# First layer of a two-layer decoder trunk: load order, x in half slices, Q/K order of two heads, and the head output on another engine

## The reference

```python
# layer 1, mLSTM: 8 heads, DK 128, DV 256, SEQ 2048, D_MODEL 2048
u = x @ w_in                                   # q,k | v | o | z | i,f gates
qk = silu(causal_depthwise_conv(qk, conv_w, conv_b))
ig, fg = split(gates + gate_b);  lf = log_sigmoid(fg)
h = mlstm_chunkwise(q, k * DK**-0.5, v, ig, lf)     # C_t = f_t C_{t-1} + i_t k_t v_t^T, running-max stabiliser
h = (h - mean(h)) * rsqrt(var(h) + eps)             # per head
h = sigmoid(o) * (h * head_g) * silu(z)
x = layernorm(ALPHA * x + h @ w_out)
# layer 2, stick-breaking attention, 16 heads of 128, K/V and Q/gate projected from x
A[t,s] = sigmoid(z_ts) * prod_{s<j<t} (1 - sigmoid(z_tj)),  s < t
x = layernorm(ALPHA * x + (A @ v * silu(z)) @ w_out)
```

## Time and profile before

| what | value |
|---|---|
| times of three runs | 2713.29, 2716.52, 2899.35 us (median 2716.52) |
| profiled execution | 2710.15 us; its slowest core's span 2708.5 us |
| PE busy | 2554.2 us (94%), 13315 matmuls |
| DVE, ACT, POOL busy | 1602.8, 970.2, 1144.7 us |
| first matmul | 25.4 us |
| last V/o/z matmuls of layer 1 start | 1055.1 us |
| out-projection of layer 1 until about | 1283 us |
| a head of layer 2 | about 72.4 us |

### The profile page before, as it was taken

How to read it: one execution, slowest core, us unless ns; L and a number is a source line. 1 busy time by engine, 2 the same in 40 slices (tenths; PEclk the granted TensorE clock), 3 DMA queues, 4 the chain that set the end, 5 groups by cost and what they waited for, 6 DMA issues and landing times.

```text
span 2708.5 us, 38664 instructions; the slowest of 8 cores (2682.8 to 2708.5 us)
## 1 busy us (share of the span) xinstructions
PE 2554.2 (94%) x13315; PEld 1279.5 (47%) x13315; DVE 1602.8 (59%) x2676; ACT 970.2 (36%) x1829; POOL 1144.7 (42%) x1127
## 2 busy tenths in 40 slices
PE   4998989998999999999889999999999999999997
PEld 2564545554555565444334444444444444444443
DVE  2654545554555554665556666666666666666665
ACT  1533434343434442322333333444444343331111
POOL 2343434343434432433444444455544544443433
PEclk9998989999999999999999999999999999999999
DMA  9847576856657357796454555455454445566851
GB/s 166 135 75 112 81 107 90 113 86 96 105 91 115 62 135 154 194 239 186 92 114 99 106 107 109 105 113 103 101 111 107 101 107 112 131 164 177 260 208 78
DMA packets 472878, 335.06 MB, mean 124 GB/s; under 512 B 413424, under 2 KB 446320, under 8 KB 461168
## 3 DMA queue, kind: packets, MB, share of 16 engines
q1 hardware_dynamic: 452128, 198.30, 31.6%
q0 software_dynamic: 20560, 134.30, 28.2%
HBM read 273.86 MB, written 92.27 MB: 135 GB/s over the span
## 4 chain that ended last, share of the span: by engine, by line
PE 73%; DVE 9%; DMA 8%; issue 4%; POOL 3%; ACT 2%; SPq 1%; another core or an unknown queue 0%; DVEq 0%; ACTq 0%; POOLq 0%
PE PSA L860 26%; PE PSA L531 19%; PE PSA L699 12%; PE PSA L482 7%; DMA mida<-REGW 6%; DVE REGW L968 6%; PE PSA L1026 4%; PE PSA L941 3%; DMA REGX<-REGW 1%; POOL REGW L724 1%; DMA REGX<-x_t 1%; DVE REGW L867 1%; SPq L161 1%; DVE REGW L509 1%; PE PSA L586 0%
## 5 line engine op out<-in xcount | busy, mean ns | idle before, releaser
L860 PE MATMUL PSA<-REGH,REGX 128*128 128x512 bf16 x4096 | 976.1, 380 | 5.7 <-DVE REGW L867 5.7
L968 DVE TENSOR_TENSOR_SCAN REGW<-PSA,REGW 128x512 f32<-128x512 f32 (+3 forms) x640 | 684.3, 1091 | 286.2 <-ACT PSA L946 236.6
L531 PE MATMUL PSA<-REGH,REGX 128*128 128x256 bf16 (+1 forms) x4096 | 718.0, 331 | 2.9 <-DMA REGH<-a_wv 2.9
L994 POOL TENSOR_TENSOR REGW<-REGW 128x1024 bf16<-128x1024 f32 (+7 forms) x384 | 527.3, 1388 | 397.6 <-DMA REGX<-REGW 197.2
L860 PEld LDWEIGHTS PSA<-REGH,REGX 128*128 128x128 bf16 x4096 | 397.3, 98 | 460.3 <-issue 10.6
L531 PEld LDWEIGHTS PSA<-REGH,REGX 128*128 128x128 bf16 x4096 | 401.2, 99 | 243.9 <-issue 24.5
L946 ACT ACTIVATE PSA<-PSA 128x512 f32<-128x512 f32 (+3 forms) x640 | 326.7, 520 | 312.2 <-PE PSA L941 307.3
L482 PE MATMUL PSA<-REGX,REGH 128*128 128x512 bf16 x1024 | 242.4, 391 | 36.9 <-DMA REGX<-x_t 29.0
L941 PE MATMUL PSA<-REGW 128*128 128x512 bf16 (+3 forms) x640 | 222.0, 349 | 27.6 <-DVE REGW L968 27.4
L509 DVE SCALAR_TENSOR_TENSOR REGW<-REGW,PRT 128x512 f32<-128x512 f32 x192 | 151.4, 791 | 157.3 <-ACT REGW L504 153.2
L872 ACT CAST REGW<-PSA 128x512 bf16<-128x512 f32 x192 | 112.7, 587 | 346.7 <-PE PSA L860 344.8
(11 more groups left out here) (115 smaller groups left out, 1990.4 us busy)
## 6 DMA issues: line engine op xcount, KB each, us to landing
REGX<-wb POOLq DMA_DIRECT2D x64, 512.0 KB, 4.9
y<-REGW SPq DMA_DIRECT2D x26, 1024.0 KB, 4.4
REGH<-a_wv POOLq DMA_DIRECT2D x32, 768.0 KB, 19.4
wb<-kv_w POOLq DMA_DIRECT2D x32, 512.0 KB, 8.7
wb<-b_w_in POOLq DMA_DIRECT2D x32, 512.0 KB, 7.3
REGW<-y SPq DMA_DIRECT2D x14, 1024.0 KB, 7.5
REGW<-x SPq DMA_DIRECT2D x13, 1024.0 KB, 5.9
REGH<-a_wqk POOLq DMA_DIRECT2D x16, 512.0 KB, 27.5
```

The costliest lines, as they stand in the source:

```text
L531: yield Op("pe", lambda: P_.matmul(PS[bank][:, 0:n1 - n0], lhsT=XT[tb][:, c, t0:t0 + 128], rhs=WV[par][:, c, n0:n1], start=(c == 0), stop= ...
L860: yield Op("pe", lambda c=c: P_.matmul(PS[bank], lhsT=WS[i % 4][:, c, :], rhs=X1[tb][:, c, :], start=(c == 0), stop=(c == KC - 1)), R=[f"W ...
L968: yield Op("dve", lambda: V.tensor_tensor_scan(out=RR[slot][:, lo:hi][:, ::-1], data0=PS[bank][:, 0:w][:, ::-1], data1=mk[:, ::-1], initia ...
L994: yield Op("pool", lambda: G.tensor_tensor(out=AA[:, (pos + b0) * 128:(pos + b1) * 128], in0=RR[slot][:, lo + 1:hi + 1], in1=RR[slot][:, l ...
```

## The change

It touches the first layer's streams and, through planner costs, the order in both layers.

- **Load order.** POOL issues the first Q weights, x slice 0 and three more Q/K weights first, and only then its constants, which become a stream `consts`. Both heads' Q/K weights precede x slices 1 to 3. The `WV` block of head 1 is loaded only after the 16 Q/K blocks of heads 0 and 1 have been through the convolution, because four more convolution buffers `U` now lie in its place.
- **x in half slices.** Each x slice is two DMAs of 1 MB with a key each.
- **Q/K order.** For heads 0 and 1 the order is x slice by x slice: q and k of head 0, then of head 1 (`border`). The gate matmuls of slice 1, 2 and 3 stand ahead of that slice's blocks.
- **Gate weight column.** Column 256 of PSUM bank 0 is set to 1.0 once; the scaling of v then covers 257 columns, and the one-column copy goes.
- **Norm weight folded.** POOL's second multiplication goes. `HB` is made by DVE, as `HN * s * HG` in one operation, instead of by ACT; there are eight `HB` buffers instead of three.
- **Planner costs** of some twenty operations change by small amounts, those of the scan and of the subtraction of layer 2 among them.

```diff
-        kb.op("pool", lambda: G.memset(ONE32[:], 1.0), W=["ONE32"])
...
-        xtk = [[("XT", i)] for i in range(4)]
+        xtk = [[("XT", i, j) for j in range(2)] for i in range(4)]
...
-        HB = [wt(0.5, [256], BF16, [("HB", i)]) for i in range(3)]
+        HB = [wt(0.5, [256], BF16, [("HB", i)]) for i in range(8)]
...
+        U += [tile("H", 40 + 2.0625 * i, [528], F32, [("U", 4 + i)]) for i in range(4)]
+
+        def consts():
+            yield lambda: at("first") >= 0
+            yield Op("pool", lambda: G.memset(ONE32[:], 1.0), W=["ONE32"], cost=0.2)
...
+            yield Op("dve", lambda: V.memset(PS[0][:, 256:257], 1.0), W=[("ps", 0)], cost=0.1)
...
+            yield lambda: at("xt") >= 3
+            yield Op("sp", None, W=["HG"], cost=2.5, dma=dict(slot="hg", out=HG, in_=a_head_g.partition_broadcast(128)))
...
             def xt(tb):
-                yield Op("pool", None, W=xtk[tb], cost=10.5, dma=dict(slot=f"xt{tb}", out=XT[tb], in_=x_t[tb]))
+                for j in range(2):
+                    yield Op("pool", None, W=[xtk[tb][j]], cost=6.2,
+                             dma=dict(slot=f"xt{tb}{j}", out=XT[tb][:, 8 * j:8 * j + 8, :], in_=x_t[tb, :, 8 * j:8 * j + 8, :]))
                 st["xt"] = tb
+            yield from wq(0, 0)
+            yield from xt(0)
             yield Op("pool", None, W=["WG"], cost=0.4,
                      dma=dict(slot="wg", out=WG.rearrange("p a b -> p (a b)"), in_=a_wg))
-            yield from wq(0, 0)
-            yield from xt(0)
-            yield from wq(0, 1)
+            for i in range(1, 4):
+                yield from wq(i // 2, i % 2)
+            st["first"] = 0
             for tb in range(1, 4):
                 yield from xt(tb)
-            yield from wq(1, 0)
-            yield from wq(1, 1)
             yield from wv(0)
+            yield lambda: len(cvd) >= 16
             yield from wv(1)
...
+        border = [(h, tb, k) for tb in range(4) for h in range(2) for k in range(2)]
+        border += [(h, tb, k) for h in range(2, NH_A) for tb in range(4) for k in range(2)]
...
-                yield Op("act", lambda: A_.activation(out=v[:, 0:256], in_=PS[0][:, 0:256], func=AF.Copy, scale=w),
-                         R=[("ps", 0), "WW"], W=[("VX", i % 4)], cost=0.42, first=True)
-                st["vev"] = i
-                yield Op("act", lambda: A_.copy(out=v[:, 256:257], in_=w), R=["WW"], W=[("VX", i % 4)], cost=0.2, first=True)
+                yield Op("act", lambda: A_.activation(out=v[:, 0:257], in_=PS[0][:, 0:257], func=AF.Copy, scale=w),
+                         R=[("ps", 0), "WW"], W=[("VX", i % 4)], cost=0.48, first=True)
...
-                yield Op("pool", lambda: G.tensor_tensor(out=gg, in0=gg, in1=HG[:, 256 * h:256 * h + 256], op=ALU.mult),
-                         R=["HG"], W=[("GG", i % 3)], cost=0.6)
...
-                yield Op("act", lambda: A_.activation(out=HB[i % 3], in_=HN[q], func=AF.Copy, scale=s(3)),
-                         R=[("HN", q), sk(3)], W=[("HB", i % 3)], cost=0.36)
-                yield Op("sp", None, R=[("HB", i % 3)], W=[("MIDA", t, h)], cost=0.5,
...
+                yield Op("dve", lambda: V.scalar_tensor_tensor(out=HB[i % 8], in0=HN[q], scalar=s(3),
+                                                               in1=HG[:, 256 * h:256 * h + 256], op0=ALU.mult, op1=ALU.mult),
+                         R=[("HN", q), sk(3), "HG"], W=[("HB", i % 8)], cost=0.5, slack=0.4)
+                yield Op("sp", None, R=[("HB", i % 8)], W=[("MIDA", t, h)], cost=0.5,
...
-                        cost=0.12 + w * 0.0022)
+                        cost=0.22 + w * 0.00209)
```

More of the change, by code:

```diff
@@ L417, in prologue @@
             for tb in range(4):
-                yield lambda: at("xt") >= tb
+                yield lambda: at("xt") >= tb and at("const") >= 0 and at("qkp") >= 4 * tb - 1
+                if tb == 0:
+                    yield lambda: at("qkp") >= 3
                 for t in range(4 * tb, 4 * tb + 4):
@@ L423, in prologue @@
                                                          start=(c == 0), stop=(c == KC - 1)),
-                                 R=xtk[tb] + ["WG"], W=[("ps", 5)], inc=(c == KC - 1 and t % 4 == 3), cost=0.05, slack=0.5)
+                                 R=[xtk[tb][c // 8], "WG"], W=[("ps", 5)], inc=(c == KC - 1 and t % 4 == 3), cost=0.05, slack=0.3)
+                st["gates"] = tb
             g3 = PS[5][:, 0:256].rearrange("p (t g) -> p t g", g=16)
@@ L472, in prologue @@
             st["pro"] = 0
+        border = [(h, tb, k) for tb in range(4) for h in range(2) for k in range(2)]
+        border += [(h, tb, k) for h in range(2, NH_A) for tb in range(4) for k in range(2)]
+        cvd = set()
         def qkp():
-            for b in range(8 * NH_A):
-                h, tb, kind = b // 8, (b % 8) // 2, b % 2
+            for b, (h, tb, kind) in enumerate(border):
                 yield lambda: (at("xt") >= tb and at("wq") >= 2 * h + kind and at("ev") >= b - 2
-                               and (h < 2 or (at("recm") >= 16 * (h - 1) - 1 and at("vz") >= 16 * (h - 1) + 2 * (b % 8) - 2)))
+                               and (h < 2 or (at("recm") >= 16 * (h - 1) - 1 and at("vz") >= b - 2 + 16 * (h - 1) - 8 * h + b - 8 * h)))
+                if b % 4 == 0 and h < 2:
+                    yield lambda: at("gates") >= tb or tb == 0
                 i = 2 * (h % 2) + kind
@@ L489, in conv @@
         def conv(kind):
-            for b in range(kind, 8 * NH_A, 2):
-                h, tb = b // 8, (b % 8) // 2
-                yield lambda: at("qkp") >= b
+            for b, (h, tb, k_) in enumerate(border):
+                if k_ != kind:
+                    continue
+                yield lambda: at("qkp") >= b and at("prt") >= 0
                 par, bank, ch = h % 2, 3 + b % 2, 8 * kind + h
-                u, p = kind + 2 * (tb % 2), kind + 2 * ((tb + 1) % 2)
+                base = 4 if h == 1 else 0
+                u, p = base + kind + 2 * (tb % 2), base + kind + 2 * ((tb + 1) % 2)
                 acc, sig, ak, gk = ACC[kind], SIG[kind], [("ACC", kind)], [("SIG", kind)]
                 wk = lambda k: PRT[:, k * 16 + ch:k * 16 + ch + 1]
-                if tb == 0 and h > 0:
+                if tb == 0 and h > 1:
                     yield Op("pool", lambda: G.memset(U[u][:, 0:3], 0.0), W=[("U", u)], cost=0.1)
@@ L519, in conv @@
                                       in_=KTa[par][:, tb * 512:(tb + 1) * 512], transpose=True))
-                st["qk" if not kind else "kk"] = 4 * h + tb
+                cvd.add((h, kind, tb))
         def vzp():
@@ L606, in recm @@
                                                           scale=DB[:, col + 8:col + 9]), R=["C32", "DB"], W=[("CB", (i + 1) % 2)],
-                             cost=0.42, first=True)
+                             cost=0.52, first=True)
                 st["recm"] = i
@@ L613, in reco @@
                 b, q, col = 5 + i % 2, i % 2, 8 * t + h
-                yield lambda: at("num") >= i and at("gg") >= i
+                yield lambda: at("num") >= i and at("gg") >= i and at("hg") >= 0
                 s = lambda j: SST[:, q, j:j + 1]
@@ L639, in reco @@
+                yield Op("sp", None, R=[("HB", i % 8)], W=[("MIDA", t, h)], cost=0.5,
+                         dma=dict(slot=f"ma{i % 8}", out=mida[t * 128:(t + 1) * 128, 256 * h:256 * h + 256], in_=HB[i % 8]))
                 st["mida"] = i
@@ L661, in amg @@
                 if t == 0:
-                    yield lambda: at("qk") >= 4 * NH_A - 1 and at("kk") >= 4 * NH_A - 1
+                    yield lambda: len(cvd) == 8 * NH_A
                     ho(*agk)
@@ L997, in sub @@
                         R=[("R", slot, c) for c in range(max(0, ci - 1), last + 1)],
-                        W=[("AA", x) for x in range(pos + b0, pos + b1)], cost=0.12 + (b1 - b0) * 128 * 0.0018)
+                        W=[("AA", x) for x in range(pos + b0, pos + b1)], cost=0.2 + (b1 - b0) * 128 * 0.00167)
                 aq.append(pos)
```

85 lines of the change are left out of this document (44 added, 41 removed).

## The result

The changed kernel takes **2624.03 us** (median of four runs; the three that are compared are 2609.03, 2619.26 and 2628.79) against 2713 to 2717 before: ratio 0.9647, 95% interval 0.956 to 0.9734, faster. The forecast was 2645 with a range of 2618 to 2684. The time lies in the range, but the gain is some 95 us where 70 were worked out, and it is made of other parts than the sum had.

The account below looks back on a forecast made before the run. The prediction took PE to bound the kernel nearly everywhere. From the profiled 2710 us it took 55 for the five stalls and 15 for the start, giving 2640, then added 5 for the faster unprofiled runs: 2645, range 2618 to 2684.

Parts of the forecast that it names:

- the planner's costs: Layer 2's matmul order shifts a little with the new costs: taken as zero gain.
- the third rival: Layer 2's new order doubles PE's waits for the scan, adding 27 us: 2672; chance 0.08.
- at best they vanish: Layer 2: the 27.4 us that PE waits for scans at best vanish, at worst double.
- The five stalls: Layer 1, one head apart: PE waits behind held-up head output writes; eight buffers gain 55 us, bounds 40.5 and 61.
- The estimate of the hold with eight buffers: Layer 1 head output writes: longest hold 30.9 us plus 6 for more weight conversions, 37 against 45 covered.
- the smaller fifth stall: Layer 1's last stall was taken as 10 us, where the others cost 12.65 each.
- the 6 us kept back for head boundaries: Layer 1: 6 of the 61 us kept, since POOL's weight issues wait for PE in both kernels.
- The moved operation: Layer 1's HB on DVE: about 0.48 us, 128 times, beside PE's work, taken as zero cost.
- The rule of the Trainium skill: A DVE operation with two SBUF inputs and a GpSimd one reading SBUF block each other; worst case 2.32 us per tile.
- The first rival: Layer 1's hold grows with the buffers past 45 to 58 us, half the gain lost: 2673; chance 0.13.
- the fourth: DVE becomes layer 1's bound if HB with waits passes 2.31 us per tile; 2773 at 3.3 us; chance 0.05.
- The start: Heads 0 and 1: slice 1 whole at 45.2, last Q/K near 96 us; 15 us gained, bounds 2 and 19.

Follow-up runs that it names:

- 1 to 4: Layer 2's new scan and subtraction costs in the kernel before: 0.9931; scan's alone 2673.28 and 2697.59 us, subtraction's alone 0.9962; old ones in the changed kernel 0.9775.
- 6: Changed kernel with the planner's cost of layer 2's scan 0.1 us lower at every width: ratio to before 0.9724.
- 10: Changed kernel in which DVE writes each head output five times over: ratio to before 0.9597, layer 1 871.8 us on core 4.
- 12: Changed kernel with the old Q/K order and head 1's weights behind the last x slice: one run left, 2620.76 us.
- 11: Changed kernel with the norm weight's load behind the first K transpose on SP's queue: ratio to before 0.9599, 2605.77 to 2615.94 us.
- experiment 1: Kernel before with only the planner costs of layer 2's scan and subtraction changed to the new ones: ratio 0.9931.
- 8: Changed kernel with three head output buffers instead of eight, the operation still on DVE: ratio to before 0.9824.

## Why the prediction was right and wrong

**The failed step is the planner's costs.** The forecast took zero for them, "since the costs move by little and towards the measured times", and priced the third rival on the other side. Layer 2 gained 28 us, all of it by the scan's cost (1 to 4). The row that points there was shown: PE's 27.4 us of waits for the scan in 48 pieces. The bound "at best they vanish" was met in size and partly by luck: 8.3 us of waits are left on core 4, and 7 us of the gain are no waits for the scan. What was left undone was to compare the planner's cost with the measured scan at each width. It shows the old cost too low at 128 to 384 columns; "towards the measured times" does not hold at 512, where the new cost moves away from them. Which of the two makes the gain stays open; that a change of 0.04 to 0.09 us in this one cost makes it is shown, and so is the loss when the cost is lowered (6).

**The five stalls** were right in place and mechanism, and so was the cure. The estimate of the hold with eight buffers, 37 us against a cover of 45, measured 38.6 on core 4 and 30.3 to 41.8 on the others. The size was short on the core that the prediction read, 63 to 66 us against 55. Five times 12.65 is 63; neither the smaller fifth stall nor the 6 us kept back for head boundaries was there. Over all cores 54 are gained, so that 55 is right for the mean, by luck: the sum was made for the slowest core.

**The moved operation** was rightly costed at nothing: 0.48 us beside PE's work, and five times as much is free as well (10). The rule of the Trainium skill that was weighed, page "SBUF — State Buffer", section "SBUF: two separate sides", on a DVE operation with two SBUF inputs beside GpSimd, would have stretched L655 had POOL been multiplying when it began. In the changed kernel that never happens: L655 stands behind POOL's power, and in none of its 128 executions on any core does a POOL operation other than the issue of a DMA run beside it, so they take 468 to 488 ns. Where the same operation does begin beside a multiplication (10) the trace agrees with the rule: 0.58 to 1.37 us in place of 0.48. So the term of zero rests on where the operation stands. The first rival is refuted (the hold grew to 41.8 at most, not past 45), and the fourth.

**The start** gained 9.4 of 15 on core 4, 9 to 11 on the six undisturbed cores. The mechanism holds (12). Slice 1 was whole at 47.7 to 49.6 over the cores and not at 45.2. Two thirds of that stand already at slice 0: reckoned from 25.4 less 2.1 it was to be whole at 23.3, and the second half came at 25.0 to 26.8, hardly earlier than the whole slice before (25.4 to 27.4). With the norm weight's load moved away it comes at 21.5 to 23.1, slice 1 at 44.1 to 46.1, and the first v matmul follows at 95 to 97 (11), where the forecast had 96 for the last Q/K. So moving that load gives back what was missing. But the 25.4 us from which the new times were reckoned held it too; why the earlier issue brought almost nothing beside it stays open.

**The rest**, 5.1 us in the out-projection and 3.7 in the tail on core 4, was forecast as nothing. The out-projection takes 222.0 to 222.2 us in the runs that keep the rest of the change, and 224 to 227 in those without (254 on two cores of experiment 1, at a granted clock of 0.88); which part of the change does it was not tried. The tail differs as much between cores as between kernels.

The table's stages add up to 2602 and not to the time, which is that of the slowest core.

## What to carry to other kernels

Where a planner writes the order of an in-order engine, set each of its costs beside the measured duration at every size before you call a change of cost nothing: an order made from costs that do not fit leaves small waits of the in-order engine, their total is in the table of waits, and here a better cost gave back about as much. A buffer that a DMA has to empty needs as many copies as the longest hold has steps of the loop; read the hold where the DMA queues are full. Moving the writing operation to another engine changed nothing about it here (8). A load that you leave where it is still has a price if what it runs beside is now on the path.
